# Ten reorderings in one tuned fp32 network kernel: mixed output groups, idle banks, norm order and pacing

## What is computed

```python
# first block: pool mixer, then latent attention
proj = rmsnorm(x) @ a_w_in                 # 2048 x 8192: values u and gate
y = (pooled(u) @ a_w_group) * scale * silu(gate)
x = x + y @ a_w_out                        # 4096 x 2048
k, v = shared_kv(x)                        # kv_w_a, then kv_w_b
proj = rmsnorm(x) @ b_w_in                 # query latent and gate
x = x + (attention(q, k, v) * silu(gate)) @ b_w_out
# second block: six modulation vectors from c, two norms
sh1, sc1, g1, sh2, sc2, g2 = split(silu(c) @ w_mod + b_mod)
h = rms_norm(x) * (1 + sc1) + sh1
qa, ka, va, qb, ckv, qi, ki, wi = split(h @ w_in)
window = sliding_window_attention(qa, ka, va, sinks, bias)     # 16 heads
picked = top_64_attention(qb, ckv, w_uk, w_uv, qi, ki, wi)     # 16 heads
x = x + g1 * (concat(window, picked) @ w_out)                  # 2048 x 2048
h = rms_norm(x) * (1 + sc2) + sh2
x = x + g2 * ((silu(conv(h @ w_up_u)) * (h @ w_up_g)) @ w_down)
out = rms_norm(x)
```

## Time and profile before

| | |
|---|---|
| median of three runs | 2118.07 us (2112.49 to 2120.44) |
| the profiled execution's own time | 2113.76 us |
| its span, first to last instruction | 2112.0 us |
| mean granted TensorE clock over the span | 0.992 of full speed |
| PE busy | 2075.8 us, 98% of the span |
| DVE busy | 1577.2 us, 75% |
| ACT busy | 1008.3 us, 48% |
| POOL busy | 54.4 us, 3% |
| weights and modulation read | 476.27 MB |

### The profile page before, as it was taken

One profiled execution on the slowest core, in us unless ns is written; L12 is line 12 of the kernel. 1 busy time (PEld: TensorE's weight loads), 2 busy tenths in 40 slices (PEclk: granted clock), 3 DMA queues, 4 the chain that ended last, 5 costly groups with the idle time before them and its releaser, 6 DMA issues.

```text
span 2112.0 us, 41562 instructions
## 1 busy us (share of the span) xinstructions
PE 2075.8 (98%) x17878; PEld 2041.3 (97%) x17878; DVE 1577.2 (75%) x2034; ACT 1008.3 (48%) x1293; POOL 54.4 (3%) x87
## 2 busy tenths in 40 slices
PE   7999999999999999999999999999999999999999
PEld 7999999999999999989999888999999999999998
DVE  7998788688577888687877798676666666666666
ACT  5444343444445476564446555454444444444443
POOL 1000000000000000000002102000000000000000
PEclk9999999999999999999999999999999999999998
DMA  7897887789676687577796664456666666666663
GB/s 251 279 351 273 307 306 270 252 290 325 210 260 178 212 287 265 176 260 252 258 347 204 217 178 140 148 168 194 195 181 207 193 194 195 183 207 192 195 194 120
DMA packets 248430, 481.13 MB, mean 228 GB/s; under 512 B 28331, under 2 KB 57623, under 8 KB 248247
## 3 DMA queue, kind: packets, MB, share of 16 engines
q1 hardware_dynamic: 247487, 478.26, 69.7%
q0 software_dynamic: 528, 0.15, 0.0%
q10 hardware_dynamic: 232, 0.06, 0.0%
HBM read 476.27 MB, written 8.44 MB: 230 GB/s over the span
## 4 chain that ended last, share of the span: by engine, by line
PE 93%; DVE 3%; issue 1%; ACT 1%; DMA 1%; POOL 0%; SPq 0%; DVEq 0%; ACTq 0%
PE acc L1797 87%; PE side L1797 3%; PE sums L1797 2%; PE sums L2074 1%; DVE w_lo L1125 1%; DMA mod_raw<-in_w_mod 1%; DVE mod_acc L1113 1%; PE acc L1904 0%; ACT prob L978 0%; ACT w_hi L629 0%; DMA x_tok<-in_x 0%; DVE m_prob L1510 0%; DMA raw<-in_b_w_out 0%; POOL prob L609 0%; PE acc L2348 0%
## 5 line engine op out<-in xcount | busy, mean ns | idle before, releaser
L1125 DVE TENSOR_TENSOR w_lo<-raw,w_hi 128x1024 fp32r<-128x1024 f32 x679 | 831.0, 1232 | 428.2 <-ACT w_hi L629 427.2
L629 ACT ACTIVATE w_hi<-raw 128x1024 fp32r<-128x1024 f32 x679 | 716.8, 1060 | 845.3 <-PE acc L1797 758.5
L1797 PE MATMUL acc<-h_hi,w_hi 128*128 128x256 f32 x3728 | 885.3, 280 | 17.6 <-issue 11.8
L1797 PE MATMUL acc<-h_lo,w_hi 128*128 128x256 f32 x3728 | 876.0, 277 | 0.0
L1797 PEld LDWEIGHTS acc<-h_hi,w_hi 128*128 128x128 f32 x3728 | 703.3, 189 | 32.1 <-issue 23.4
L1797 PEld LDWEIGHTS acc<-h_lo,w_hi 128*128 128x128 f32 x3728 | 703.4, 189 | 0.3 <-issue 0.2
L1797 PE MATMUL acc<-h_hi,w_lo 128*128 128x256 f32 x3728 | 502.4, 277 | 0.0
L1797 PEld LDWEIGHTS acc<-h_hi,w_lo 128*128 128x128 f32 x3728 | 460.4, 188 | 0.0
L1113 DVE SCALAR_TENSOR_TENSOR mod_acc<-mod_raw,silu_c,mod_acc 128x1024 f32<-128x1024 f32 x180 | 230.9, 1283 | 11.2 <-DMA mod_raw<-in_w_mod 11.2
L1797 PE MATMUL acc<-f_hi,w_hi 128*128 128x256 f32 x704 | 164.3, 276 | 0.0
L1797 PE MATMUL acc<-f_lo,w_hi 128*128 128x256 f32 x704 | 164.1, 276 | 0.0
(11 more groups left out here) (320 smaller groups left out, 2041.8 us busy)
## 6 DMA issues: line engine op xcount, KB each, us to landing
mod_raw<-in_w_mod SPq DMA_DIRECT2D x192, 512.0 KB, 5.9
raw<-in_w_up SPq DMA_DIRECT2D x176, 512.0 KB, 4.4
raw<-in_a_w_in SPq DMA_DIRECT2D x128, 512.0 KB, 5.1
raw<-in_w_down SPq DMA_DIRECT2D x88, 512.0 KB, 4.4
raw<-in_a_w_out SPq DMA_DIRECT2D x64, 512.0 KB, 5.0
raw<-in_w_in SPq DMA_DIRECT2D x56, 512.0 KB, 4.1
raw<-in_b_w_in SPq DMA_DIRECT2D x40, 512.0 KB, 4.7
raw<-in_a_w_group SPq DMA_DIRECT2D x32, 512.0 KB, 5.4
```

The lines of the kernel that those rows point to most:

```text
L629: last = act.activation(w_hi[s][:, :], raw[s][:, :], ACT.Copy)
L1125: last = dve.tensor_tensor(w_lo[s][:, :], raw[s][:, :], f32(w_hi[s][:, :]), ALU.subtract)
L1797: return pe.matmul(o, lhsT, rhs, start=start, stop=stop, skip_group_check=True)
```

## The change

Ten edits, all of order or place; no product is computed differently in value except that some squares are added before they are summed.

1. `first_slab`: for the first slab of the program, of `w_in` and of the feed-forward part, PE does the 8 products of `w_hi` with the high half, then 8 of `w_lo`, then 8 of `w_hi` with the low half, and waits for each when it comes to it.
2. ACT's `root` comes two splits earlier; ACT splits slabs 339, 340 (and 433, 434) after parts 0 and 1. DVE's `norm_root` comes right after the last add; its splits of 338 to 340 (432 to 434) come after the low halves of parts 0, 1 and 2.
3. DVE folds tiles 2, 3 of the added squares onto tiles 0, 1 (one addition more), so PE sums 12 products where it summed 16 (and 24 small ones where it had 32 at the end).
4. In the last pair ACT's `m_hi(0, 2)` comes before `m_silu` and the split of slab 305; DVE's `m_low(0, 2)` comes before `m_soft`.
5. `MOD_PACE`: (314, 148), (324, 148) give way to (306, 134): one tile every second slab from 294 to 306, and no pause from 314 to 324.
6. The adds of the latent attention's output come one slab earlier, at 18, 19, 27, 33 behind `OUT_AT`; those of `w_out` at 26, 27, 31, 33 behind `MIX_AT`.
7. Keys: tiles 0 to 3 accumulate in `sums`, 4 to 7 in `acc`; values: half 0 in `side`, half 1 in `acc`. Before, both kinds took both sets of `acc`. A new semaphore `home_taken` says that `sums` and `side` were read.
8. `w_out`: column groups 2 and 3 accumulate over window and picked heads without being read between; groups 0 and 1 have their picked half last. The slabs are loaded in that order. Two of DVE's adds (four instructions of L1246 each) fall away.
9. The squares of the second norm are taken in the order of tiles 8, 12, 0, 4.
10. At the very end `turn_out(2)` stands inside the last slab's products, between its second and third column block.

The diff, cut to its core:

```diff
 MOD_PACE = (...
-            (294, 128), (314, 148), (324, 148), (336, 160), (341, 160), (363, 176), (385, 186), (396, 192))
+            (294, 128), (306, 134), (336, 160), (341, 160), (363, 176), (385, 186), (396, 192))
...
-            def h_split(shift=None):
+            def h_split(shift):
                 for j in range(KD // 2):
                     h_part(j, shift)
+                    if j < 2:
+                        split(1)
...
+                if last:
+                    act.wait_ge(slab_used, done.value(RING))
+                    m_hi(0, 2)
                 if n % 2:
                     m_silu(n - 1)
                 split_to(at + 5)
                 m_stage_k(n % 2)
-                if last:
-                    m_hi(0, 2)
...
-            split_to(OUT_AT + 36)
-            sq_adds.step(2)
+            split_to(OUT_AT + 34)
+            sq_adds.step(3)
             root()
             h_split(0)
...
+            s = product(2)
+            act.activation(kb[:, 0:4, :], sums_tiles, ACT.Copy).then_inc(home_taken, 1)
+            taken(act.activation(kb[:, 4:8, :], acc[s][:, :, :], ACT.Copy))
...
                 for j in range(KD // 2):
                     low(j)
+                    if j < 3:
+                        split(1)
                     if j + 2 < KD // 2:
                         scaled(j + 2)
...
+                if m == 2:
+                    dve.wait_ge(sq_added, sq_adds.value())
+                    sq_adds.step()
+                    dve.tensor_tensor(tmp[0][:, 0:2, :], tmp[0][:, 0:2, :], tmp[0][:, 2:4, :], ALU.add).then_inc(sq_added, 1)
...
+                if last:
+                    m_low(0, 2)
                 if n:
                     m_soft()
...
-                split_to(OUT_AT + (19, 20, 28, 33)[m])
+                split_to(OUT_AT + (18, 19, 27, 33)[m])
                 add_product((15, 1, 8, 8)[m], 4 * m, tail=m == 3)
...
-            split_to(OUT_AT + 36)
             norm_root()
...
-                if q % 2 == 0 and q < TILES:
+                if q in (0, 2):
                     add_product(4, 2 * q, scale=2)
...
-                split_to(MIX_AT + (27, 28, 32, 33)[m])
-                add_product((7, 1, 4, 4)[m], 4 * m, scale=2, tail=m == 3)
+                split_to(MIX_AT + (26, 27, 31, 33)[m])
+                add_product((15, 1, 4, 4)[m], (8, 12, 0, 4)[m], scale=2, tail=m == 3)
...
+            def first_slab(a, hi, lo, x_hi, x_lo, k, ready):
+
+                pe.wait_ge(h_hi_ready, ready + 1)
+                for x, (w, starts) in ((x_hi, (hi, True)), (x_hi, (lo, False)), (x_lo, (hi, False))):
+                    if w is lo:
+                        pe.wait_ge(lo_ready, slabs.value(RING + 1))
+                    if x is x_lo:
+                        pe.wait_ge(h_lo_ready, ready + 1)
+                    for i in range(4):
+                        for kk in range(k):
+                            last = mm(a[:, i, :], w[:, kk, i * P:(i + 1) * P], x[:, kk, :], start=starts and i % 2 == 0 and kk == 0)
+                last.then_inc(slab_used, 1)
+                slabs.step()
...
-                sum_squares(4, rms_sum, tmp[0], True, False)
+                sum_squares(2, rms_sum, tmp[0], True, False)
...
-            for m in range(4):
+            for m in range(2):
                 gemm(4, h_hi, h_lo, four, before=windowed)
+            both = [gemm(8, h_hi, h_lo, four, before=windowed, parts=range(4)) for m in range(2, 4)]
...
+            for parts in ((4, 5), (6,), (7,)):
+                for a in both:
+                    gemm(8, h_hi, h_lo, four, before=selected, a=a, parts=parts)
+            for m in range(2):
+                gemm(4, h_hi, h_lo, four, x0=TILES, tail=m == 1)
...
-            gemm(2, f_hi[0], f_lo[0], four, a=a, parts=(1,), tail=True)
-            pe.wait_ge(sq_added, sq_adds.value(2))
+            gemm(2, f_hi[0], f_lo[0], four, a=a, parts=(1,), tail=True, between=lambda: turn_out(2, acc_banks[macros.slot(2)]))
+            pe.wait_ge(sq_added, sq_adds.value(3))
             pe.wait_ge(y_copied, 1)
-            token_squares(tmp[0], 4, True, False)
+            token_squares(tmp[0], 2, True, False)
```

More of the change, by code:

```diff
@@ L1834, in gemm @@
                     lo = w_lo[w][:, 0:k * n].rearrange("p (k n) -> p k n", k=k)
+                    if first is not None and s == 0:
+                        pe.wait_ge(hi_ready, slabs.value(1))
+                        first_slab(a, hi, lo, x_hi, x_lo, k, first)
+                        continue
                     if before:
@@ L1973, in _ @@
                 for m in range(2):
-                    gemm(8, h_hi, h_lo, four, before=h_ready(0))
+                    gemm(8, h_hi, h_lo, four, before=h_ready(0), first=0 if g == 0 and m == 0 else None)
                     if g == 0 and m == 0:
@@ L2263, in _ @@
             for m in range(3):
-                gemm(8, h_hi, h_lo, four, before=h_ready(24))
+                gemm(8, h_hi, h_lo, four, before=h_ready(24), first=24 if m == 0 else None)
             for m in range(2):
@@ L2284, in _ @@
                 slabs.step()
-            sets = [set_free()]
+            pe.wait_ge(idx_relu, TILES)
+            homes = [side]
             for r in range(2):
@@ L2325, in _, with ff_up @@
             ffs = Count()
-            def ff_up(before=None):
-                for m in range(2):
-                    gemm(8, h_hi, h_lo, four, before=before)
+            def ff_up(before=None, first=None):
+                gemm(8, h_hi, h_lo, four, before=before, first=first)
+                gemm(8, h_hi, h_lo, four, before=before)
             def ff_down(a):
```

83 lines of the change are left out of this document (37 added, 46 removed).

## The result

| kernel | executions | median | lowest to highest | over 2130 us |
|---|---|---|---|---|
| before | 20 | 2115.27 us | 2111.87 to 2151.30 | 2 |
| changed | 20 | 2140.57 us | 2111.61 to 2149.49 | 15 |

The changed kernel is slower: 2140.57 / 2115.27 = 1.0120 by the medians. The comparison that leaves out executions more than 1.5% above a kernel's fastest gives 1.0063, 95% interval 1.0036 to 1.0090; as that bound cuts through the changed kernel's larger group, the two groups are told apart here in full. Sorted, the changed kernel's executions are

What follows compares the result with a forecast made beforehand. PE, busy 98%, was taken as the bound, leaving 36 us idle and half-clock stretches. Terms 0.55 − 1.5 + 1.95 + 0.3 + 3.3 + 0.4 + 1.9 = 6.9 us; 2118.1 − 6.9 = 2111.2, said as 2111, range 2102 to 2118.

Steps and rivals of the forecast that it cites:

- the norm of slab 431: Second norm: reciprocal 1.64 us earlier, three splits moved into the parts; +0.4 us of PE's 2.6 gained at the start.
- the second rival: PE's new waits at slabs 341 and 435 each bring half clock, 1.4 to 2.5 us; 2114.5 us, chance 0.15.
- Slab 305 and the pacing: Slabs 305 to 321: wait and half clock at 305 go, a new 4 us wait at 321 takes the gain; −1.5 us.
- The rival by which DVE keeps up: Add for slab 321 done before slab 320 ends, so the 4.3 us stay; 13.9 us gain, 2104, chance 0.22.
- the rival with late tiles: Eight mod tiles in nine slabs land late, slab 321 12 us later than counted; 2123 us, chance 0.05.
- Norm of slab 337: First norm: PE starts 3.5 us earlier, then waits ahead of slab 341 for 1.5 to 4 us; +1.95 us.
- Keys and values: Their waits go, but busy DVE and the picked attention a few slabs later absorb most; +0.3 us, at most 3.1.
- `w_out`: Output product: the 1.8 and 1.3 us waits at slabs 417 and 423 go; +3.3 us, bounds 1.8 and 3.6.
- The rival that it would be absorbed: `w_out` gain lost because PE's next need is late: 3.3 us less, 2114.5 us, chance 0.08.
- First slab: Start of the program: PE starts 0.73 us earlier, half lost if the clock rises no sooner; +0.55 us.
- End: Fewer last sums save 1.2 us; `turn_out(2)` moves into the last slab, costing 1.0; +1.9 us, bounds 1.2 and 2.3.
- the rule that I had weighed against the trace: Applied at slab 321: a long idle gap brings the slow clock again; by it the term is −1.5, without it 0.

Runs made afterwards that it cites:

- Experiments 1: Changed kernel with the norm at slab 431 ordered as before: median 2113.26 us, 2 of 12 over 2130.
- 2: Kernel before with one added wait, ACT splitting slab 435 only once PE has finished slab 434: median 2140.83 us, 7 of 12 over 2130.
- experiment 3: Changed kernel with a one-column fp32 product ahead of slabs 436 and 444: median 2114.1 us, 0 of 11 over 2130.
- experiment 4: Changed kernel with the old table of mod tiles: 6 of 12 over 2130 us, the six others with median 2107.7 us.
- experiment 8: Changed kernel with the norm at slab 337 ordered as before: one profiled execution, 2143.1 us.
- 5: Kernel before with ACT splitting slab 500 only once PE has finished slab 499: 0 of 11 over 2130; groups 2112.5 to 2117.1 and 2120.9 to 2122.8 us.
- 6: Kernel before with a one-column fp32 product ahead of slabs 436 and 444, no added wait: median 2114.4 us, 0 of 11 over 2130.
- 9: Changed kernel with the old table of mod tiles and one-column fp32 products ahead of slabs 436 and 444: median 2108.2 us, ratio 0.9943 to the kernel before.
- 12: Changed kernel with a second wait, ACT splitting slab 437 only once PE has finished slab 436, no small product: median 2141.1 us, 8 of 12 over 2130.
- 7: Changed kernel with old mod-tile table, old norm order at 431 and one-column fp32 products ahead of slabs 436 and 444: median 2108.5 us, ratio 0.9960 to before.

## Why the prediction was wrong

The forecast was 2111 us, range 2102 to 2118; the median came out at 2140.6. Its base, 2118.1, was a median of three; twenty executions of the kernel before gave 2115.3. By its own steps:

**The step that failed** is the norm of slab 431, "+0.4 of the 2.6 us that PE gains at the start". The mechanics were as said: the reciprocal came earlier, PE gained 2.3 us at slab 431, and lost it again, 0.9 in slabs 431 and 432, where more products now fell into the stretch of half clock, and 1.4 at the late split of 435 (from slab 430 to slab 436 the net is 0.0). What the step had no price for is the state in which a wait leaves PE. I had priced a wait at its own length and at a stretch of half clock (the second rival, 1.4 to 2.5 us). No half clock followed: the granted clock stays at 1.00 through slab 694. The price was 259 slabs x 0.107 = 27.7 us, in three of four executions, because behind slab 435 nothing interrupts the row of equal work for 700 us. Experiments 1 and 2 show it from both sides. That the wait stands at the head of this row does not explain it alone: the kernel before waits 2.3 us at slab 431, ahead of the same row, and only 22 of the 136 executions without a wait at 435 were over 2130. Why a wait at 435 is followed by the slow pace so much more often stays open.

The sign of it was in the trace of before. Slabs 317 to 320 stand at 117.8 ns there, so that slab 319 takes 2.83 us where others take 2.72, and the forecast used 2.8 in the count for DVE without asking why.

**Slab 305 and the pacing (−1.5 forecast).** The long wait at 305 went, and the half clock behind it: 3.52 and 1.49 us by slab 306, forecast 3.5 and 1.4. But the half clock had only moved. A new wait for the low half, 0.99 us, stands ahead of slab 307, some small products follow it, and slab 307 then runs at half clock (the window's columns as in the earlier trace rows):

```profile
936.85 0.87 PE L2103 MATMUL sums<-table,m_prob 128*128 128x128 f32 x6 [0.99 <-DVE h_lo L1545]
938.95:942.36 3.41, 3.41 (x18) 3.41 (x18) 3.41 (x4) 2.12 (x3) 0.00 (x0) 0.50 0.05 14
```

Together they took 2.8 us up to slab 308, where I had forecast about 1 for the wait and nothing for the clock. From slab 301 to slab 309 the five profiles with the new table gained 1.0 to 2.6 us, not 4.3. The wait for the first add came as forecast, 3.40 us (forecast about 4). The net from slab 301 to 321 was −1.1 in the changed kernel's profile. No half clock followed there, which I had counted in; instead two waits for `w_lo` at 335 and 336 took 1.7, which makes −2.8. In the profile of experiment 3 it did follow, and the net to slab 325 was −5.6. So the sign was right and the size 1 to 4 us too small. By experiment 4 the new table costs 4.7 us to slab 321. The rival by which DVE keeps up fell; of the rival with late tiles the mechanism showed weakly (DVE waited 15.4 us for tiles in all, before 11.2).

**Norm of slab 337 (+1.95).** PE starts 3.42 us earlier (3.5 forecast), then waits 2.2 at slab 341; net 1.8 from slab 336. Right, and confirmed by experiment 8 with 1.7.

**Keys and values (+0.3).** 3.1 us gained between slabs 390 and 399, all of it given back by slab 408 (waits for `a_neg`, 1.5, and for POOL's `prob`). Net 0.0. The absorption was right.

**`w_out` (+3.3).** 1.88 at slab 417 and 1.38 at 423, 3.26 together. Right. The rival that it would be absorbed fell.

**First slab (+0.55).** Between 0.06 and 1.33 at slab 9 in the ten profiles with this edit, against the one profile in the earlier trace rows; the three other profiles with the old order stand 0.1 to 0.5 behind that one. The clock rises at 20.3 us in the profile with 1.33 and at 22.7 in one with 0.06.

**End (+1.9).** From the start of slab 694 to the end of the span it is 15.4 us instead of 16.5: 1.1. But the kernels of experiments 2, 5 and 6 have the old end too and take 15.2 to 15.3, so the 16.5 was high for the old order and a saving is not shown. The products of slab 694 take 0.8 us longer with `turn_out(2)` between them (forecast 1.0), and what follows them takes 11.7 us instead of 12.5 in those three. The last chain also has ACT and the output's store in it; what takes up the rest of the forecast's saving was not traced.

The sum over all terms without the two slow stretches (5.7 and 27.7 us) is 29.0 − 33.4, that is 4.4 us faster in this profile; in that of experiment 3, without its slow stretch of 1.9, it is 0.5 faster. Forecast: 6.9 faster. The lower group, 2115.2 against 2114.7, says that at the quick pace the change is worth about nothing, and experiments 4 and 9 say that the table took what the rest brought: with the old one 7 us are there. That is more than the 4.7 by slab 321; where the rest arises was not traced.

Three readings in the forecast were off by a little. The window that holds 32 products at full clock has 20 of 128 columns among them; the 1.4 us taken from it measured 1.49. The 4.98 and 4.52 us of half clock hold 44 and 40 products at 113.3 ns, not 47 and 42, so they cost 2.4 and 2.0 us. And PE, 4.3 us ahead of the 985.56 at which its wait for slab 321 began, would have wanted that slab at 981.3, not 981.9. None of them changes the sum.

On the clock, the rule that I had weighed against the trace, in the Trainium skill's page "TensorE: Matmul & The Clock Gate", section "HAM oscillation — how this bites in real kernels", is that an idle gap long enough costs full speed each time anew. The trace agrees with it in part. The wait of 3.40 us at slab 321 was followed by PEclk 1.00 in the changed kernel's profile. In those of experiments 3, 8 and 12 the same wait, 3.40 us at the same slab, came with 0.50 for 6.8, 3.4 and 6.8 us, and the wait of 0.99 us ahead of slab 307 had half clock behind it, too, though small products stood between. The measurement decides: here a wait may cost the clock, and need not, and its length alone does not say which. The step of the forecast from waits of 1.8 and 2.3 us to a limit between them does not hold.

## What to carry to other kernels

Before moving work so that a wait disappears, ask where the next wait will stand and what runs behind it. A wait is not always worth its own length: the one at the head of 259 slabs of equal work cost 28 us in most executions here. With small products of another kind behind it, some 0.2 us each, it cost that in none of 21 executions. If a kernel's times fall into two groups, count the matmuls in a window in which PE is busy throughout, at the same granted clock, in both. Time a change of under one per cent over enough executions to see both groups, and keep background work off the engine that the next free accumulator waits for.

## What was not expected of the hardware

**Two paces at one granted clock.** The same product, 128x128 by 256 columns, starts every 113.3 ns or every 117.8 ns (885 or 851 in 100 us), with PEclk at 1.00 both times. Once PE has a pace it keeps it for as long as equal products follow, over 730 us here. What decides between them is open. Shown is: the pace ahead of an interruption need not be that behind it. By the times, a wait of 1.0 to 1.2 us at slab 435 was followed by the slow pace in 36 of 56 executions and one at slab 500 by the quick one in 11 of 11; with fp32 products of one column ahead of slabs 436 and 444 it was the quick one in 63 of 63. By the profiles, the one at 436 ended the slow pace twice (7 and 9), and in four more PE was quick already. Why the small product does so, and whether another instruction would, was not tried.

**Half clock is not certain behind a wait, and not only long waits have it.** The wait of 3.40 us at slab 321 was followed by none in the changed kernel's profile, by 3.4 us of it in that of experiment 8, and by 6.8 in those of 3 and 12. A wait of 0.99 us ahead of slab 307 was followed by six products of 128 columns, twelve of one or two columns and then 3.4 us of half clock. What decides was not tried.
